# Output projection of the second block computed by heads inside the last attention, a second buffer of transposed probabilities, and squares added by VectorE

## The reference

```python
o_nsa = gates[..., 0:1] * o_cmp + gates[..., 1:2] * o_slc + gates[..., 2:3] * o_win
o_nsa = rms_norm_2(o_nsa.reshape(B, S, NSA_HEADS * HEAD_DIM), nsa_out_norm)
o_swa = banded_attention(qw, kw, v_sw, SWA_WINDOW, swa_sinks)
o_swa = rms_norm_2(o_swa.reshape(B, S, SWA_HEADS * HEAD_DIM), swa_out_norm)
mixed = jnp.concatenate([o_nsa, o_swa], axis=-1) @ w_out
h = h + rms_norm_2(mixed, attn_post_norm)
hn = rms_norm_2(h, ffn_pre_norm)
```

## Time and profile before

| | us |
|---|---|
| median of three runs | 1269.61 (1269.0 to 1271.76) |
| the profiled execution, its own time | 1268.81 |
| its span in the profile | 1267.0 |
| TensorE busy | 1192.4 (94%) |
| VectorE busy | 910.2 (72%) |
| ScalarE busy | 604.0 (48%) |
| GpSimd busy | 100.3 (8%) |

### The profile page before, as it was taken

The page is one execution under the profiler, slowest core; times in us unless marked ns, Lnnn a source line. Parts: engine busy times, 40 slices in busy tenths (PEclk is TensorE's granted clock), DMA queues, the critical chain, the costliest instruction groups (busy, mean ns, idle before and its releaser), DMA issues.

```text
span 1267.0 us, 24166 instructions
## 1 busy us (share of the span) xinstructions
PE 1192.4 (94%) x9202; PEld 1132.9 (89%) x9202; DVE 910.2 (72%) x1517; ACT 604.0 (48%) x1027; POOL 100.3 (8%) x77
## 2 busy tenths in 40 slices
PE   8999999999999999999999999999968897999996
PEld 8988898999999999679899999999945597999996
DVE  7999885766656586657757666558887467999855
ACT  5663644444444543435445444454355434666541
POOL 1575010100000000001000000002000000000000
PEclk9999999999999999999999999999987888999998
DMA  7554342445555456134424555555550022445562
GB/s 270 171 195 148 119 167 100 167 166 190 174 190 190 155 197 216 34 123 145 166 101 167 169 195 169 196 200 180 198 198 16 1 68 100 166 169 195 181 217 68
DMA packets 32457, 197.51 MB, mean 156 GB/s; under 512 B 3712, under 2 KB 7936, under 8 KB 9472
## 3 DMA queue, kind: packets, MB, share of 16 engines
q1 hardware_dynamic: 30752, 194.14, 44.2%
q10 hardware_dynamic: 1632, 2.36, 0.5%
HBM read 193.08 MB, written 1.05 MB: 153 GB/s over the span
## 4 chain that ended last, share of the span: by engine, by line
PE 74%; DVE 16%; ACT 5%; issue 3%; DMA 1%; DVEq 0%; ACTq 0%; SPq 0%
PE acc L476 19%; PE acc L478 19%; PE acc L477 18%; PE acc L512 7%; DVE wlo L1275 3%; DVE wlo L1268 3%; PE acc L492 2%; PE acc L773 2%; ACT whi L905 2%; DMA raw<-weights 1%; PE sc L737 1%; PE tp L476 1%; PE tp L762 1%; DVE nw L1324 1%; DVE nw L1323 1%
## 5 line engine op out<-in xcount | busy, mean ns | idle before, releaser
L476 PE MATMUL acc<-Hhi,whi 128*128 128x256 f32 x1376 | 391.4, 284 | 7.9 <-DVE wlo L1275 7.6
L477 PE MATMUL acc<-Hlo,whi 128*128 128x256 f32 x1376 | 389.4, 283 | 0.0
L478 PE MATMUL acc<-Hhi,wlo 128*128 128x256 f32 x1376 | 389.3, 283 | 0.0
L905 ACT ACTIVATE whi<-raw 128x1024 fp32r<-128x1024 f32 x163 | 172.1, 1056 | 334.0 <-PE acc L478 312.8
L1268 DVE TENSOR_TENSOR wlo<-raw,whi 128x1024 fp32r<-128x1024 f32 x164 | 206.5, 1259 | 115.0 <-ACT whi L905 113.0
L476 PEld LDWEIGHTS acc<-Hhi,whi 128*128 128x128 f32 x1376 | 264.0, 192 | 11.6 <-DVE wlo L1275 8.2
L477 PEld LDWEIGHTS acc<-Hlo,whi 128*128 128x128 f32 x1376 | 264.1, 192 | 0.1
L478 PEld LDWEIGHTS acc<-Hhi,wlo 128*128 128x128 f32 x1376 | 264.1, 192 | 0.0
L476 PE MATMUL acc<-FH,whi 128*128 128x256 f32 x848 | 240.5, 284 | 11.8 <-DVE wlo L1275 7.0
L478 PE MATMUL acc<-FH,wlo 128*128 128x256 f32 x848 | 238.8, 282 | 0.0
L1275 DVE TENSOR_TENSOR wlo<-raw,whi 128x1024 fp32r<-128x1024 f32 x164 | 204.7, 1248 | 1.3
(11 more groups left out here) (273 smaller groups left out, 1770.5 us busy)
## 6 DMA issues: line engine op xcount, KB each, us to landing
raw<-weights SPq DMA_DIRECT2D x177, 1024.0 KB, 4.9
MEM<-mem_in SPq DMA_DIRECT2D x2, 1024.0 KB, 7.4
held<-weights SPq DMA_DIRECT2D x2, 1024.0 KB, 5.8
E<-A ACTq DMA_DIRECT2D x14, 128.0 KB, 2.9
X<-x_in SPq DMA_DIRECT2D x4, 256.0 KB, 3.7
raw<-weights SPq DMA_DIRECT2D x2, 512.0 KB, 6.9
out<-X SPq DMA_DIRECT2D x4, 256.0 KB, 2.1
cst<-consts SPq DMA_DIRECT2D x1, 998.0 KB, 11.2
```

Of the source, the lines that this page charges most:

```text
L476: pe.matmul(dst, w, x, start=first, stop=False)
L477: pe.matmul(dst, w, xl, start=False, stop=False)
L478: return pe.matmul(dst, wl, x, start=False, stop=last)
L905: act.activation(whi[j][:, 0:HALF, :], raw[j][:, 0:HALF, :], ACT.Copy).then_inc(hi_out, 1)
```

## The change

- **Squares.** GpSimd adds only the first norm's squares. In the six residuals VectorE adds the second pair of each round to the first as soon as ScalarE has squared it (behind the low half, ahead of the halving), and behind the loop the sum of round 2 to that of round 1; in down1 it does so for two sets. TensorE's sums wait for `pairs_joined`. One memset stays on GpSimd.
- **Second buffer.** Transposed probabilities of NSA units alternate between PT and a part of MEM; a copy waits for the values two units back.
- **Projection by heads.** The norms of the two halves are no longer applied ahead. ScalarE and VectorE make Ohi and Olo of each pair of heads as its attention ends, unscaled but for the gains. The products of the four SWA pairs (96 instructions) run in six pieces, `swa_part(0)` to `(5)`: 12 instructions each behind steps 14, 15, 16 and 17 into one half of PSUM tile st, which ScalarE empties in steps 15 to 18, and two of 24 in step 19 into sc. The products of the four NSA pairs are `nsa_part(0)` to `(3)`, 24 instructions each. VectorE multiplies them with the quotient of the two norms (R), adds the SWA part, and the second norm goes into the factor of the norm behind. The filler products go. Tiles 2 and 3 of the weights go to buffers of their own and are halved in steps 4 to 9. Five of the group sums move to step 18, three behind the pieces of step 19.
- **Behind it.** The first tile of up2 is halved behind the last sum, ahead of the norm; gains are applied with the norm's factor.

```diff
+        with ExitStack() as shared:
+            KVr = sb("KVr", [P, 4 * DC, S], F32R, shared)
         MKV = sb("MKV", [P, 4 * DC, S])
...
+        turned_of = [PT, MEM[:, 0:4, :].rearrange("p (b a) s -> p b (a s)", b=2)]
+        halves = lambda bank: bank.rearrange("p (a b) -> p a b", a=2)
+        late_part = {2: halves(sc[:, 2, :]), 3: halves(sc[:, 3, :])}
+        out_sums = [halves(sc[:, 0, :]), halves(sc[:, 1, :]), acc[0][:, :, :], acc[1][:, :, :]]
+        out_weights = [(whi[0], wlo[0]), (whi[1], wlo[1]), (Hhi, Hlo),
+                       (KVr[:, 8:16, :], KVr[:, 24:32, :])]
...
-        SUMMED = ["mix0", "mem0", "ffn0", "attn1", "mem1", "ffn1", "final", "pre2"]
+        SUMMED = ["mix0"]
+
+        joined = Steps(pairs_joined, [("mem0", 3), ("ffn0", 3), ("attn1", 3), ("mem1", 3), ("ffn1", 3), ("final", 2), ("pre2", 2 + 2)])
+        JOINED_BEHIND = {"pw2": "mem0", "memo0": "ffn0", "down0": "attn1", "diffo": "mem1", "memo1": "ffn1", "down1": "final"}
...
-            for name in SUMMED[1:]:
-                sum_squares(name)
-                if name == "ffn0":
-                    pool.memset(E[:, :, :, :], 0.0).then_inc(turned_zero, 1)
+            pool.wait_ge(s_sq, sq.at("memo0"))
+            pool.memset(E[:, :, :, :], 0.0).then_inc(turned_zero, 1)
...
                             pe.wait_ge(squares_summed, SUMMED.index(of) + 1)
+                        elif of in joined.first:
+                            pe.wait_ge(pairs_joined, joined.at("pre2", 3) if of == "final" else joined.at(of))
                         else:
                             pe.wait_ge(s_sq, sq.at(SQ_OF[of]))
...
+                    while summed < 8 and s >= ends[summed] + 7 and (name == "attn_diff" or s == 18):
...
+            LAST_UNIT = U0["attn_nsa"] + len(ATTN["attn_nsa"]) - 1
+
+            def heads_part(t, heads, dst, ms=range(2)):
+
+                hi, lo = out_weights[t]
+                tile_in(L0["wout"] + t)
+                for k, c in enumerate(heads):
+                    for m in ms:
+                        o = slice(m * P, (m + 1) * P)
+                        mm = three(dst[:, m - ms[0], :], hi[:, c, o], lo[:, c, o], Ohi[:, c, :], Olo[:, c, :],
+                                   k == 0 and m == ms[0], k == 3 and m == ms[-1])
+                return mm
+
+            def swa_part(n):
+
+                if n == 0:
+                    pe.wait_ge(s_h, h.at("outn", 4))
+                if n < 4:
+                    if n:
+                        pe.wait_ge(part_taken, n)
+                    heads_part(n // 2, (4, 5, 6, 7), st[:, S:2 * S].unsqueeze(1), (n % 2,)).then_inc(part_done, 1)
+                else:
+                    pe.wait_ge(exp_done, LAST_UNIT)
+                    heads_part(n - 2, (4, 5, 6, 7), late_part[n - 2]).then_inc(part_done, 1)
+
+            def nsa_part(t):
+
+                if t < 2:
+                    pe.wait_ge(exp_done, LAST_UNIT + 1)
+                elif t == 2:
+                    pe.wait_ge(acc_free, G0["wout"] + 2)
+                else:
+                    pe.wait_ge(pt_ready, LAST_UNIT + 1)
+                if t == 0:
+                    pe.wait_ge(s_h, h.at("outn"))
+                heads_part(t, (0, 1, 2, 3), out_sums[t]).then_inc(tile_done, 1)
+
             pe.wait_ge(acc_free, G0["attn_nsa"] + 2)
-            attention("attn_nsa", {3: turn_hidden, 5: compressed, 8: lambda: pe.wait_ge(cmp_ready, 1)})
-            meanwhile(5)
-            spread("out2", [(2 * b + tt, sc[:, 0, b * S + tt * P:][:, 0:P]) for b in range(2) for tt in range(NT)])
+            attention("attn_nsa", {3: turn_hidden, 5: compressed, 8: lambda: pe.wait_ge(cmp_ready, 1)},
+                      between={14: (0,), 15: (1,), 16: (2,), 17: (3,), 19: (4, 5)}, between_step=swa_parts)
+            sums_behind = token_sums("post2", "wout")
             row_of_tokens = [(tt, sc[:, 0, tt * P:(tt + 1) * P]) for tt in range(NT)]
-            meanwhile(7)
-            stage("wout", Ohi, Olo, source="outn", behind=token_sums("post2", "wout"))
+            nsa_part(0)
+            pe.wait_ge(pt_ready, LAST_UNIT + 1)
+            spread("out2", [(4 + tt, tp[:, tt * P:(tt + 1) * P]) for tt in range(NT)])
+            for t in range(1, 4):
+                nsa_part(t)
+            sums_behind(2)
...
-                        act.wait_ge(pv_done, values_done(n - 1))
+                        act.wait_ge(pv_done, values_done(n - 2))
                         for b, bank in enumerate((tp[:, :], second_tp)):
-                            to, frm = (t.rearrange("p (m k) -> p m k", m=2)[:, :, 0:u["keys"]] for t in (PT[:, b, :], bank))
+                            to, frm = (t.rearrange("p (m k) -> p m k", m=2)[:, :, 0:u["keys"]] for t in (turned_of[n % 2][:, b, :], bank))
...
+                            if name == "attn_nsa":
+                                act.activation(Ohi[:, to, :], A[:, slot, :], ACT.Copy, scale=C("g_out2", to, 1)).then_inc(s_taken, 1)
                             act.activation(SQ[:, to, :], A[:, slot, :], ACT.Square).then_inc(s_sq, 1)
...
-            attention("attn_nsa")
-            ready_chunks("outn", A[:, Q_SLOT:Q_SLOT + 8, :], Ohi, "g_out2", squares=False)
-            residual("wout", 2, [])
+            def piece(n):
+
+                act.wait_ge(part_done, n + 1)
+                act.activation(M2[:, n, :], st[:, S:2 * S], ACT.Copy).then_inc(part_taken, 1)
+
+            attention("attn_nsa", {**{4 + 2 * (t - 2) + half: lambda t=t, half=half: out_weight_half(t, half)
+                                      for t in (2, 3) for half in range(2)},
+                                   **{15 + n: lambda n=n: piece(n) for n in range(4)}})
+            up = 16 * (T0["up2"] // 2 + 1)
+            split(up, 0, T0["wout"] + 1)
+            for t in range(4):
+                acc_out("wout", t)
+                act.activation(pair(SQ, 2 * t), pair(M2, 2 * t), ACT.Square).then_inc(s_sq, 1)
+                if t == 1:
+                    split(up, 1, T0["wout"] + 2)
...
+            def out_weight_half(t, half):
+
+                k = slice(half * HALF, (half + 1) * HALF)
+                dve.wait_ge(hi_out, 2 * split_before(T0["wout"] + t) + half + 1)
+                ins = dve.tensor_tensor(out=out_weights[t][1][:, k, :], in0=raw[t % 2][:, k, :], in1=f(out_weights[t][0][:, k, :]),
+                                        op=ALU.subtract)
+                if half:
+                    ins.then_inc(lo_dve, 1)
...
+                            if g and name in JOINED_BEHIND:
+                                dve.wait_ge(s_sq, 2 * i + sq.at(name, 2))
+                                for q in (SQ, SQF) if name == "down1" else (SQ,):
+                                    dve.tensor_tensor(out=pair(q, 4 * i), in0=pair(q, 4 * i), in1=pair(q, 4 * i + 2), op=ALU.add)\
+                                        .then_inc(pairs_joined, 1)
                             if g and not (name == "wout" and start):
                                 weights(ks[-1:])
+                if name == "down1":
+                    dve.wait_ge(pairs_joined, joined.at("pre2", 2))
+                    for q in (SQ, SQF):
+                        dve.tensor_tensor(out=q[:, 0:2, :], in0=q[:, 0:2, :], in1=q[:, 4:6, :], op=ALU.add).then_inc(pairs_joined, 1)
+                elif name in JOINED_BEHIND:
+                    dve.wait_ge(pairs_joined, joined.at(JOINED_BEHIND[name], 2))
+                    dve.tensor_tensor(out=SQ[:, 0:2, :], in0=SQ[:, 0:2, :], in1=SQ[:, 4:6, :], op=ALU.add).then_inc(pairs_joined, 1)
...
+                def out_rest(s):
+                    if name == "attn_nsa" and 6 <= s and units[s - 6]["last"]:
+                        g, slot = units[s - 6]["group"], units[s - 6]["slot"]
+                        to = slot - Q_SLOT
+                        dve.wait_ge(s_taken, taken.at("outn", g + 1))
+                        dve.scalar_tensor_tensor(out=Olo[:, to, :], in0=A[:, slot, :], scalar=C("g_out2", to, 1),
+                                                 in1=f(Ohi[:, to, :]), op0=ALU.mult, op1=ALU.subtract).then_inc(s_h, 1)
...
-            attention("attn_nsa", {4: copy_hidden, 6: compressed})
-            norm_columns("out2", 4, D // 2, RMS_EPS)
+            attention("attn_nsa", {4: copy_hidden, 6: compressed,
+                                   **{(5, 7, 8, 9)[2 * (t - 2) + half]: lambda t=t, half=half: out_weight_half(t, half)
+                                      for t in (2, 3) for half in range(2)}})
+            factors = rt[:, RT["out2"], :]
+            first, second, quotient, second2 = (factors[:, 2 * k:2 * k + 2] for k in range(4))
+            link(inverse_root("out2", 4, D // 2, RMS_EPS, factors[:, 0:4]))
+            link(dve.reciprocal(quotient, second))
+            dve.tensor_tensor(out=quotient, in0=first, in1=quotient, op=ALU.mult).then_inc(rt_ready, 1)
+            link(dve.tensor_tensor(out=second2, in0=second, in1=second, op=ALU.mult))
```

(45 more changed lines are left out.)

47 lines of the change are left out of this document (30 added, 17 removed).

## The result

| | before | after |
|---|---|---|
| median of 5 runs beside each other, us | 1269.61 (1267.85 to 1274.18) | 1261.44 (1258.25 to 1261.98, and one run of 1937.86) |
| ratio to before, 95% interval | | 0.9923 [0.9901, 0.9944] |
| profiled execution: own time, span, us | 1268.81, 1267.0 | 1261.98, 1260.2 |

The kernel became 0.8% faster, 9.8 us by the ratio and 8.2 by the medians. The forecast was 1258.1 with a range of 1253.5 to 1266.0. The median lies in the range, 3.3 us above the forecast. The run of 1937.86 us had a granted clock of 0.585; it counts in the median and not in the ratio, and the median of the other four is 1259.95.

A forecast was written before the change was run, and what follows sets the result against it. TensorE was taken as the bound, busy 1192.4 of 1267.0 us. Terms -1.7 +1.7 -14.25 +1.8 +0.8 = -11.65, called -11.5: profiled 1257.3, median 1258.1; own range 1253.5 to 1262.5, to 1266.0 with all rivals but the slower one.

The forecast's parts named there:

- squares: Six stages: VectorE adds squares instead of GpSimd; halvings shorten, some sums come later; -1.7 us, bounds +2.0 and -4.3.
- attention to step 14: Last attention up to step 13: added halvings delay step 10's maximum and the softmax; +1.7 us, bounds 0 and +4.3.
- step 14 to the last product: Last attention's end and projection: filled waits, full clock, shorter norm path, less three added group sums; 58.0 to 43.75, -14.25 us.
- behind the projection: Last product to up2's first product: extra multiply, halving ahead of the norm, short steps, scaled products; +1.8 us.
- clock reserve: Last attention: half of the 1.75 us lost to half clock in one stretch, kept as reserve; +0.8 us, bounds 0 and +8.
- I give it -1.4 of the 2.0: Behind down1: VectorE's chain gets 2.0 us shorter without GpSimd's additions, and TensorE's waits there gain 1.4 of it.
- Some 2.0 of its 2.55 idle can take them: Steps 7 to 9: 4.3 us of added VectorE work, 2.0 fits idle time, so step 10's maximum comes 2.3 later.
- What should have shown it: Signs across the kernel; wrong if step 14 to last product exceeds 50 us or step 10's maximum comes over 4 later.
- The pieces hold the softmax up: Last attention: step 16's scores stand behind a piece, all 5.2 us of waits stay, VectorE's delay is maximal; 1263.5, chance 0.15.
- The clock falls as before: Last attention: the sixteen us at half clock stay, 8.0 us of lost work less 0.8; 1265.3, chance 0.10.
- GpSimd's additions were not what drew VectorE out: Residual stages: moved squares only add work and delays, +3.5 us instead of -1.7; 1263.3, chance 0.08.
- Half clock for the whole projection: Steps 9 and 10's long wait halves the clock, pieces don't restore it; all 44 us at half, 1279, chance 0.07.

The follow-up runs named there:

- experiment 5: The changed kernel with three VectorE halvings of output weights moved late, from steps 7 to 9 to steps 15, 16 and 18: 1259.26 us, ratio 0.9917.
- heads alone: The changed kernel with GpSimd adding the squares as before, so only the output projection's part of the change: 1259.67 us, ratio 0.9917.
- experiment 9: The kernel before with unread filler products in two TensorE waits of the last attention, 4 in step 15 and 9 in step 17: 1266.24 us, ratio 0.9962.
- Experiment 8: Changed kernel, last squares addition ahead of last halving, group sums together, pieces 0 to 3 moved from steps 14 to 17 into step 19: 1262.64 us, ratio 0.9932.
- experiments 6: Changed kernel with the last squares addition ahead of the last halving, but one buffer of transposed probabilities instead of two: 1254.45 us, ratio 0.9875.
- experiment 1: The kernel before with only the additions of squares moved from GpSimd to VectorE: 1271.49 us, ratio 0.999.
- experiment 7: Changed kernel with the last squares addition ahead of the last halving, and all eight group sums behind the last piece: 1254.52 us, ratio 0.9873.

## Why the prediction was right, and where it was not

| term | forecast | measured | by what |
|---|---|---|---|
| squares | -1.7 | +0.7 (-0.2 with more profiles, below) | to the attention, 809.2 to 809.9; alone 0.999 [0.997, 1.0011] |
| attention to step 14 | +1.7 | +2.5 in the trace, of which 0.3 to 1.4 can be the halvings' | 45.0 to 47.6; experiment 5 and the kernels beside it |
| step 14 to the last product | -14.25 | -12.3 | 58.0 to 45.7 |
| behind the projection | +1.8 | +1.8 | 9.9 to 11.7 |
| clock reserve | +0.8 | (in the second row) | |

They make -7.3; with 0.6 us that the trace after lost ahead of the 135-us mark, -6.7, which is what up2's first product moved (1056.68 to 1049.94).

**Squares: 2.4 us off on this trace, of which the stage of win is shown.** The mechanism was right: GpSimd drew VectorE out, halvings fell to 1.22, and the first rounds gained. The delays of the sums at memq0 and memq1 came too (waits of 1.10 and 0.82), and up to gu1's sums the forecast (-0.3) and the trace (+0.1) agree, as far as single traces tell: the same code differs by 1 us there. The step that failed is "I give it -1.4 of the 2.0" for win. I had costed the last addition behind the halvings at the memory queries, and forgot it in the one stage where two additions stand last. There TensorE waited 1.92, and the clock fell behind it, 1.6 us more. This stage can be compared in six profiles: from gu1's sums to the attention's start the three kernels with GpSimd's additions (before, heads alone, fillers in before) take 274.5 to 274.8, and the three with the change's (after, squares alone, halvings late) 274.9 to 275.4, each with a wait of 1.92 or 1.94 and a fall behind it. That is +0.5 for a forecast -1.4. To the attention in all, the means of the same three and three are 0.2 apart (809.7 and 809.5), so the whole part is 1.5 to 2.4 us off.

**Attention: the term of +1.7 was too large, and its size in the trace was chance.** "Some 2.0 of its 2.55 idle can take them. So the maximum of step 10 ... comes 2.3 later" is the step. In the kernel after that maximum starts 33.9 us after the attention does, 3.4 later than before, and no longer waits:

```profile
978.85 1.22 DVE L1697 TENSOR_REDUCE mx<-sc 128x4 f32<-128x1024 f32 x1
```

But in experiment 5, with three halvings gone from there, it still comes 32.1 after the start, beside 32.5 in the heads-alone kernel and 30.5 before. Kernels with these halvings in place reach step 14 in 44.1 to 49.3 us, kernels without them in 45.0 to 51.1, and the order within each group is that of the mean clock (0.85 at 44.1, 0.66 at 49.3, 0.64 at 51.1). At the same clock the halvings cost 0.3 to 1.4: in the heads-alone kernel that maximum comes 2.0 later than before, near the forecast 2.3, but from it to step 14 are 13.1 us where 14.5 were, so that 1.4 come back and not 0.6. The trace of the kernel after showed 2.5 us and seemed to confirm the term; only other kernels told that most of it was chance. That is the main lesson of this case on method.

**Steps 14 to 19: right, 1.9 too much.** The waits gave 4.1 (5.2 to 1.1) for a forecast 3.4. The clock of the attention held as the forecast said, and experiment 9 gives it a price of its own, 4.7 us with a later fall taken off, beside 5.5. But it was not all gain: the new burst of group sums brings the clock down for 4 us, some 1.7 lost. The forecast took the three group sums that come in at 0.45 each, and did not see what five in a row do. That is most of the 1.9. Experiment 8 prices the pieces: 6.5 us, a fall of the clock for 3 us included. One reason named was wrong: the second buffer does nothing for TensorE (experiments 6 and 8).

**Behind the projection: right to a tenth.** A chain of instructions of known length, with nothing beside it, can be summed from rows.

**What should have shown it.** Most signs came true: no halving above 1.3 us from 150 us on, the clock at 1.00 in the steps with pieces, the stretch at 45.7 for 42 to 46, and 11.7 from there to up2. The waits for low halves fell by 7.6 and not by some 4, but the new waits for the additions took that back. The maximum of step 10 came 3.4 us later; 4 would have meant that the forecast was wrong.

**The rivals.** "The pieces hold the softmax up": no, one wait of 1.11 is left. "The clock falls as before": no in the attention, yes for 4 us behind the group sums. "GpSimd's additions were not what drew VectorE out": no, experiment 1. "Half clock for the whole projection": no, it lasted 4 of 44 us.

The Trainium skill (TensorE: Matmul & The Clock Gate, HAM oscillation) says that bursts between waits can start throttled each time. The traces agree that it happens, but not each time: the wait at 405 is 1.92 to 2.45 in six profiles and the clock fell in five; it is 1.73 in eight, and the clock fell in two.

## What to carry to other kernels

When work moves to a busier engine's queue, count at every stage what it stands behind there, and put the piece that another engine needs first ahead of the piece that it needs later: here that order was worth 2.6 to 5 us, and the move nothing that could be measured. Price a wait by what the clock does behind it, too. A wait filled with useful products can gain more than its own length, and here even useless ones gained 4.7 us (experiment 9). And don't take a difference of 2 us in a latency-bound stretch from one trace of each kernel: look at it in kernels that don't differ there, and compare at the same granted clock.

## What was not expected of the hardware

- The clock fell with no wait near it behind a burst of products of one column: 0.57 to 0.60 for 4 us behind 20 to 32 of them, at a new place when they moved (experiment 7). Twelve in a row at 1024.59 in the kernel after, with full products around them, left it at 1.00.
- The same code with the same wait has its clock fall in some executions and not in others (the wait of 1.92 at 405: 1.00 in one profile, 0.60 in others, 2.0 us apart). It can make part of the spread of these kernels: before ran from 1266.6 to 1279.5 in 17 runs of one comparison.
- Fillers begun after the fall did not bring the clock back within the gap (0.50 from 1033 to 1039 under 12 fillers, 1.00 from 1039.5), while with fillers ahead of the place of the fall it stayed (1.00 in experiment 9).
- Writing a VectorE loop of two rounds out shortened waits behind it by 0.2 to 0.3 us each (0.50 to 0.21 at 165, 1.93 to 1.73 at 405).
